# First feed-forward product: its weights in four blocks, with another order on SyncE, GpSimd and ScalarE

## The reference

```python
h = (rmsnorm(x, P['g_pre_ffn'][l]) * (1.0 + scale2) + shift2).astype(x.dtype)
up = h @ P['w_up'][l]                                  # 1024 -> 5632
up, ffn_conv_new = causal_dwconv(up, ffn_conv_prev, P['ffn_conv_w'][l])   # 3 taps
a, b = jnp.split(up.astype(f32), 2, axis=-1)
y = (jax.nn.gelu(a) * b).astype(x.dtype) @ P['w_down'][l]
```

## Time and profile before

| | |
|---|---|
| three runs | 1896.59, 1900.85, 1907.34 us; median 1900.85 |
| profiled execution | 1898.44 us, its span 1896.7 us |
| busy in the span | TensorE 1630.2, VectorE 946.4, GpSimd 737.6, ScalarE 591.9 us |
| granted TensorE clock, mean | 0.922 |
| largest GpSimd group | `lo`, L2433, 84 of 128x512 from the sums, mean 1536 ns |

### The profile page before, as it was taken

The page is one execution under the profiler, slowest core; times in us unless marked ns, Lnnn a source line. Parts: engine busy times, 40 slices in busy tenths (PEclk is TensorE's granted clock), DMA queues, the critical chain, the costliest instruction groups (busy, mean ns, idle before and its releaser), DMA issues. The chain is left out here.

```text
span 1896.7 us, 27581 instructions
## 1 busy us (share of the span) xinstructions
PE 1630.2 (86%) x10719; PEld 1426.4 (75%) x10719; DVE 946.4 (50%) x1601; ACT 591.9 (31%) x1003; POOL 737.6 (39%) x925
## 2 busy tenths in 40 slices
PE   5799988999788777998796589999999995999997
PEld 2568886899566545897674589988899995778886
DVE  1551027630556444454344856666666665555553
ACT  2431132221344341232243243333333332332322
POOL 1531022221100027853023777777777773211111
PEclk7899988999799977897898789999999998999999
DMA  8425422230311067321331111111111111855562
GB/s 322 139 90 202 141 88 82 70 94 33 103 59 45 18 216 183 81 97 34 139 109 58 54 57 69 69 69 68 69 69 69 69 69 55 271 201 196 201 221 108
DMA packets 123043, 208.09 MB, mean 110 GB/s; under 512 B 37492, under 2 KB 85668, under 8 KB 119586
## 3 DMA queue, kind: packets, MB, share of 16 engines
q1 hardware_dynamic: 120450, 197.42, 31.8%
q10 hardware_dynamic: 2464, 8.91, 1.2%
HBM read 163.26 MB, written 42.91 MB: 109 GB/s over the span
## 5 line engine op out<-in xcount | busy, mean ns | idle before, releaser
L2645 DVE SCALAR_TENSOR_TENSOR fu_tmp<-fu_zp,fu_cw,fu_tmp 128x1024 f32<-128x1024 f32 x88 | 121.8, 1384 | 176.3 <-ACT fu_tmp L2579 174.7
L2400 PE MATMUL fu_ps<-fu_thi,fu_whi 128*128 128x272 f32 (+2 forms) x672 | 144.8, 298 | 38.0 <-DVE fu_zp L2662 38.0
L2872 PE MATMUL fd_ps<-fd_whi,fd_yhi 128*128 128x512 f32 x396 | 123.6, 394 | 25.5 <-DVE fd_wlo L2926 20.8
L2400 PE MATMUL fu_ps<-fu_tlo,fu_whi 128*128 128x272 f32 (+2 forms) x672 | 143.5, 296 | 0.0
L2400 PE MATMUL fu_ps<-fu_thi,fu_wlo 128*128 128x272 f32 (+2 forms) x672 | 143.1, 295 | 0.0
L2400 PEld LDWEIGHTS fu_ps<-fu_thi,fu_whi 128*128 128x128 f32 x672 | 110.9, 195 | 41.8 <-POOL fu_wlo L2433 41.2
L2433 POOL TENSOR_TENSOR fu_wlo<-fu_s,fu_whi 128x512 fp32r<-128x512 f32 x84 | 128.1, 1536 | 12.8 <-ACT fu_whi L2535 12.8
L2889 ACT ACTIVATE fd_whi<-fd_w 128x1024 fp32r<-128x1024 f32 x66 | 69.9, 1060 | 186.8 <-PE fd_ps L2872 148.0
L2433 POOL TENSOR_TENSOR fu_wlo<-fu_w,fu_whi 128x512 fp32r<-128x512 f32 x67 | 119.4, 1784 | 9.4 <-ACT fu_whi L2535 9.4
L2872 PE MATMUL fd_ps<-fd_wlo,fd_yhi 128*128 128x512 f32 x396 | 123.0, 392 | 0.0
L2400 PE MATMUL fu_ps<-h_hi,fu_whi 128*128 128x272 f32 (+1 forms) x504 | 105.7, 291 | 14.9 <-POOL fu_wlo L2433 14.9
(11 more groups left out here) (358 smaller groups left out, 3828.8 us busy)
## 6 DMA issues: line engine op xcount, KB each, us to landing
fd_w<-in_w_down SPq DMA_DIRECT2D x66, 512.0 KB, 4.8
wa<-in_w_ada SPq DMA_DIRECT2D x24, 1024.0 KB, 6.5
fu_w<-in_w_up SPq DMA_DIRECT2D x44, 512.0 KB
scr_y<-fu_tmp SPq DMA_DIRECT2D x22, 544.0 KB, 2.7
fd_y<-scr_y SPq DMA_DIRECT2D x44, 192.0 KB
fp_w<-in_w_fm SPq DMA_DIRECT2D x16, 512.0 KB, 3.7
scr_qkv<-fp_y SPq DMA_DIRECT2D x9, 512.0 KB, 2.9
dr_stg<-scr_qkv SPq DMA_DIRECT2D x8, 576.0 KB, 5.9
```

The lines of the kernel that those rows point to most:

```text
L2400: last = pe.matmul(lane_of(q, o)[:, n, 0:size], w[:, o, kk], part(low, kk, slice(c, c + size)), start=(kk == 0 and m == 0), stop=(kk == HK ...
L2645: one = dve.scalar_tensor_tensor(yp, a, w, yp, ALU.mult, ALU.add)
L2872: last = pe.matmul(ps[OUT_BANK[p][n]][:, c:c + 512], y[:, k, n * P:(n + 1) * P], w[:, k, c:c + 512], start=(f == 0 and m == 0), stop=(f == ...
```

## The change

The buffer of raw weights and four semaphores, one per block, are made before `output_projection`, and SP issues the four loads (256 KB each) of unit 0 at the end of its list there. In `ffn_up` every block is loaded by itself, with a wait for its own last reader. The sums and parts get the order A11, S3, S2, S1, A12, S4, A22 on GpSimd and ScalarE; TensorE keeps its order of products and waits for the place of its operand in the new one (`split_at`). `first_tap(j,0)` moves ahead of the high part of S4.

```diff
@@ output_projection, SP, after the last load of x
+            for m in range(2):
+                for k in range(2):
+                    c = slice(KD // 2 * k, KD // 2 * (k + 1))
+                    sp.dma_start(K.w_up_raw[:, m, c], K.w_up_d[m, :, c]).then_inc(K.w_up_in[2 * m + k], 16)
@@ ffn_up
+        ORDER = (A11, S3, S2, S1, A12, S4, A22)
+        raw11_in, raw12_in, raw21_in, raw22_in = K.w_up_in
+        def split_at(j, o):
+            return splits(j) + (ORDER0 if j == 0 else ORDER).index(o) + 1
...
-            def load(j):
-                after(sp, lo_set, splits(j))
-                for m in range(2):
-                    sp.dma_start(raw[:, m], K.w_up_d[2 * j + m]).then_inc(raw_in, 16)
+            def load(j, m, k):
+                sp.dma_start(raw[:, m, HK * k:HK * k + HK], K.w_up_d[2 * j + m, :, HK * k:HK * k + HK])\
+                    .then_inc(K.w_up_in[2 * m + k], 16)
+
+            def load_front(j):
+                if j == 1:
+                    sp.wait_ge(lo_set, split_at(0, A21))
+                else:
+                    sp.wait_ge(lo_set, split_at(j - 1, A11))
+                    sp.wait_ge(s_set, 4 * (j - 1) - 1)
+                load(j, 0, 0)
+                load(j, 1, 0)
+
+            def load_back(j):
+                sp.wait_ge(lo_set, split_at(j - 1, A12))
+                if j > 1:
+                    sp.wait_ge(s_set, 4 * (j - 1))
+                load(j, 0, 1)
+                sp.wait_ge(lo_set, split_at(j - 1, A22))
+                load(j, 1, 1)
 
             def store(j):
                 sp.wait_ge(y_set, j + 1)
                 sp.dma_start(K.scr_y[j], ybuf(j)).then_inc(K.y_kept[j % 2], 16)
 
-            load(0)
             sp.dma_start(prev[:], K.fprev_d).then_inc(small_in, 16)
             sp.dma_start(cw[:], K.fconv_d).then_inc(small_in, 16)
-            load(1)
-            for j in range(KF):
-                if 0 < j < KF - 1:
-                    load(j + 1)
-                if j:
-                    store(j - 1)
+            load_front(1)
+            load_back(1)
+            for j in range(1, KF):
+                if j + 1 < KF:
+                    load_front(j + 1)
+                store(j - 1)
+                if j + 1 < KF:
+                    load_back(j + 1)
...
             def front_sums(j):
-                pool.wait_ge(raw_in, 32 * (j + 1))
-                pool.wait_ge(lo_set, splits(j))
+
+                if j > 1:
+                    pool.wait_ge(lo_set, split_at(j - 1, S2))
+                    pool.wait_ge(s_set, 4 * (j - 1))
+                pool.wait_ge(raw11_in, 16 * (j + 1))
+                pool.wait_ge(raw21_in, 16 * (j + 1))
+                pool.tensor_tensor(sums[:, 1], a11, a21, ALU.subtract).then_inc(s_set, 1)
+                if j > 1:
+                    pool.wait_ge(lo_set, split_at(j - 1, S4))
+                pool.wait_ge(raw22_in, 16 * (j + 1))
                 pool.tensor_tensor(sums[:, 0], a21, a22, ALU.add).then_inc(s_set, 1)
-                pool.wait_ge(s_set, 4 * (j - 1) + 1)
+
+            def middle_sum(j):
+                pool.wait_ge(lo_set, split_at(j, S3))
+                pool.wait_ge(s_set, 4 * (j - 1) + 2)
                 pool.tensor_tensor(sums[:, 1], sums[:, 0], a11, ALU.subtract).then_inc(s_set, 1)
 
-            def back_sums(j):
-                pool.wait_ge(lo_set, splits(j) + S1 + 1)
-                pool.wait_ge(s_set, 4 * (j - 1) + 2)
+            def back_sum(j):
+                pool.wait_ge(lo_set, split_at(j, S1))
+                pool.wait_ge(s_set, 4 * (j - 1) + 3)
+                pool.wait_ge(raw12_in, 16 * (j + 1))
                 pool.tensor_tensor(sums[:, 0], a12, sums[:, 1], ALU.subtract).then_inc(s_set, 1)
-                pool.wait_ge(s_set, 4 * (j - 1) + 3)
-                pool.tensor_tensor(sums[:, 1], a11, a21, ALU.subtract).then_inc(s_set, 1)
...
             for j in range(1, KF):
                 more = j + 1 < KF
-                if more:
-                    front_sums(j + 1)
                 halo(j, 0)
                 if more:
                     lo(j + 1, A11)
+                    front_sums(j + 1)
+                    lo(j + 1, S3)
+                    middle_sum(j + 1)
                     lo(j + 1, S2)
                     lo(j + 1, S1)
-                    back_sums(j + 1)
+                    back_sum(j + 1)
                 halo(j, 1)
-                if more:
-                    lo(j + 1, S3)
                 copies(j, 1)
                 if more:
                     lo(j + 1, A12)
-                    lo(j + 1, S4)
                 copies(j, 0)
                 if more:
+                    lo(j + 1, S4)
                     lo(j + 1, A22)
...
-            high(0)
             hi(0, A11)
             hi(0, A12)
+            high(0)
             high(1)
             hi(0, A21)
             hi(0, A22)
...
                 first_tap(j - 1, 1)
                 gelu(j - 1)
                 if more:
-                    for o in (A11, S2, S1, S3, A12, S4):
+                    for o in (A11, S3, S2, S1, A12):
                         hi(j + 1, o)
                 first_tap(j, 0)
                 if more:
+                    hi(j + 1, S4)
                     hi(j + 1, A22)
```

More of the change, by code:

```diff
@@ L2270, in ffn_up @@
         SPLIT = {A11: EVEN, S2: EVEN, S1: EVEN, S3: BACK, A12: EVEN, S4: BACK, A22: EVEN}
-        raw = sb("fu_w", [P, 2, KD, P])
+        raw = K.w_up_raw
         w_hi = sb("fu_whi", [P, PROD, HK, P], F32R)
@@ L2283, in ffn_up @@
         ps = [own.enter_context(nc.psum_tensor(f"fu_ps{i}", [P, 2, 512], F32)) for i in range(4)]
-        (raw_in, small_in, hi_set, lo_set, s_set, f_set, td, th_set, l4_set, mm0, mm, tap_set, e0_set, p1_set, c11_set, u2_set, u3_set, u4_set, c22_set,
+        (small_in, hi_set, lo_set, s_set, f_set, td, th_set, l4_set, mm0, mm, tap_set, e0_set, p1_set, c11_set, u2_set, u3_set, u4_set, c22_set,
          c12_set, c21_set, chain_s, conv_a_set, conv_b_set, gelu_set, y_set, zero_set, halo_a, halo_b, copied_a, copied_b,
          st_out) = (sem("fu_" + n) for n in (
-             "raw_in small_in hi_set lo_set s_set f_set td th_set l4_set mm0 mm tap_set e0_set p1_set c11_set u2_set u3_set u4_set c22_set "
+             "small_in hi_set lo_set s_set f_set td th_set l4_set mm0 mm tap_set e0_set p1_set c11_set u2_set u3_set u4_set c22_set "
              "c12_set c21_set chain conv_a_set conv_b_set gelu_set y_set zero_set halo_a halo_b copied_a copied_b "
@@ L2390, in product @@
             def product(q, o, part):
-                pe.wait_ge(lo_set, splits(q + 1) + o + 1)
+                pe.wait_ge(lo_set, split_at(q + 1, o))
                 lane_free(q, o)
@@ L2430, in lo @@
             def lo(j, o):
-                n = splits(j) + (ORDER0.index(o) if j == 0 else o)
-                pool.wait_ge(hi_set, n + 1)
+                pool.wait_ge(hi_set, split_at(j, o))
                 pool.tensor_tensor(w_lo[:, o], block_of(j, o), w_hi[:, o], ALU.subtract).then_inc(lo_set, 1)
             def front_sums(j):
-                pool.wait_ge(raw_in, 32 * (j + 1))
-                pool.wait_ge(lo_set, splits(j))
+                if j > 1:
[7 more added lines that the diff above has]
+                pool.wait_ge(raw22_in, 16 * (j + 1))
                 pool.tensor_tensor(sums[:, 0], a21, a22, ALU.add).then_inc(s_set, 1)
-                pool.wait_ge(s_set, 4 * (j - 1) + 1)
+            def middle_sum(j):
+                pool.wait_ge(lo_set, split_at(j, S3))
+                pool.wait_ge(s_set, 4 * (j - 1) + 2)
                 pool.tensor_tensor(sums[:, 1], sums[:, 0], a11, ALU.subtract).then_inc(s_set, 1)
-            def back_sums(j):
-                pool.wait_ge(lo_set, splits(j) + S1 + 1)
-                pool.wait_ge(s_set, 4 * (j - 1) + 2)
+            def back_sum(j):
+                pool.wait_ge(lo_set, split_at(j, S1))
+                pool.wait_ge(s_set, 4 * (j - 1) + 3)
+                pool.wait_ge(raw12_in, 16 * (j + 1))
                 pool.tensor_tensor(sums[:, 0], a12, sums[:, 1], ALU.subtract).then_inc(s_set, 1)
-                pool.wait_ge(s_set, 4 * (j - 1) + 3)
-                pool.tensor_tensor(sums[:, 1], a11, a21, ALU.subtract).then_inc(s_set, 1)
             def whole(c):
@@ L2490, in _ @@
             lo(1, A11)
+            lo(1, S3)
+            middle_sum(1)
             lo(1, S2)
             lo(1, S1)
-            back_sums(1)
-            lo(1, S3)
+            back_sum(1)
             lo(1, A12)
@@ L2524, in hi @@
             def hi(j, o):
-                if o in (A11, A12, A22) or j == 0:
-                    act.wait_ge(raw_in, 32 * (j + 1))
+                if j == 0:
+                    act.wait_ge({A11: raw11_in, A12: raw12_in, A21: raw21_in, A22: raw22_in}[o], 16)
+                elif o in (A11, A12, A22):
+                    act.wait_ge({A11: raw11_in, A12: raw12_in, A22: raw22_in}[o], 16 * (j + 1))
                 else:
-                    act.wait_ge(s_set, 4 * (j - 1) + {S1: 1, S2: 2, S4: 3, S3: 4}[o])
```

(7 more changed lines are left out.)

## The result

Slower: 1974.11 us (median of 4 runs, 1968.91 to 1976.19) against 1899.04 before; ratio 1.038, 95% interval 1.034 to 1.042. The prediction was 1952 in 1912 to 1984. The profiled execution took 1976.19, its span is 1974.4: 77.7 more than before.

The account below looks back on a forecast made before the run. The prediction took GpSimd's work plus one bare load to bound the old kernel's round. Twenty rounds at 26.5 make 530 us (+53.5); with +2 and -2, 1898.4 becomes 1952, range 1912 to 1984.

Parts of the forecast that it names:

- The ring: Steady rounds: a22's load queues behind store(j-1), which waits for VectorE's product(j-1); this closes a loop of 26.5 us a round.
- rival D: Steady rounds: a22 arrives in time, GpSimd never waits, TensorE's 21.27 us sets the round; 1847 us, chance 0.03.
- fixed terms: Steps of one round besides landing and convolutions: 3.9, 1.58, 1.40, 0.79, 1.42, 1.45 and 1.28 us.
- rival B: Steady rounds: everything collides, product too, or blocks land at 5.7; rounds of 27.2 to 29, 1966 to 2002 us, chance 0.18.
- The landing: SP's store and two back loads after product, until a22 can be used: 4.85 us, bounds 3.5 to 5.7.
- The convolutions: VectorE's two convolutions per round, slowed by turns with GpSimd: 9.8 us together, 6.1 if free.
- values of before: The two convolutions' times in the old kernel's trace, 5.29 and 3.96, 9.25 us together; a round of 25.9.
- TensorE's clock: TensorE in steady rounds: some show a halved clock, at no cost unless more than 5.2 us is lost.
- Start and end: Before product(0): +2 us (bounds -4 to +4); after product(20), with TensorE further ahead: -2 us (bounds -4 to 0).
- The Trainium skill's estimate: Landing of the back blocks: last 256 KB about 3.4 us after product, a round of 25.1, the time 1924 us.

Follow-up runs that it names:

- the run with the wait alone: Changed kernel where SP still waits for product(j-1) ahead of the back blocks, but issues the store itself behind them: 1958.57 us, ratio 1.033.

## Why the prediction was right

- **The ring** was the step that decided, and it is shown: open it and the time falls to 1847, close it in the old kernel and that one slows by 9%. That 1847 is also rival D's figure is partly luck: D had rounds of 21.27 and put nothing outside them; measured were rounds of 20.97, and 9.5 us more outside them.
- **Its fixed terms** held to 0.1: 3.9 from the sum with a22 to the high part of S2 (1395.88 to 1399.78), 1.57 to the tap, 1.41 to the convolution, 0.80 and 1.42 around the second tap, 1.44 and 1.28 at the end (1389.10 gives 1390.38).
- **The band.** The measured round, 27.63, and time lie not in the band named the forecast (25.9 to 27.2, 1940 to 1966, chance 0.45) but in rival B's (27.2 to 29, 1966 to 2002, chance 0.18). B asked for all steps to collide, `product` too, or for blocks landing at 5.7. Neither came in full: `product` took 1.28 as before. The mechanism was right, and two of its terms were too small:
- **The landing**: 4.85 forecast, 5.37 (median) measured. In the turn shown a22, the third DMA in a row, took 0.79 to issue, twice what I counted. That this makes the difference is argued, not shown; a22 issued before a12 landed at 4.76.
- **The convolutions**: 9.8 forecast, 3.97 + 6.53 = 10.5 (medians). Laid out by turns I had 4.25 + 5.85 = 10.1, and I took less than my own layout. In the second, I left out S3's sum, the one just before GpSimd waits for a22: the trace shows four collisions, with the low parts of S4 (1408.34), A22 (1409.60) and A11 (1411.97) and with that sum (1413.22). My "values of before", 9.25, came from one round whose second convolution took 3.96; the median of the 20 rounds is 2.92, so that value should have been 8.2. Together with the landing this is 1.2 a round; the round was 27.63 where 26.5 was forecast, 23 us in all, nearly the whole of the difference between 1952 and the profiled execution's 1976.
- **TensorE's clock** cost nothing, as forecast. It fell around the waits of 3 to 4 us, and TensorE's busy time in the 20 rounds rose from 438.5 to 467.8 us, to 23.4 a round. That is still under 27.63, and VectorE, which is on the ring, waited for TensorE 0.3 us in all.
- **Start and end**: forecast +2 and -2, measured +0.9 (1111.55 against 1110.63) and +0.6 (from the last of these products to the end 310.2 against 309.6). TensorE began at 1046.33 in place of 1053.87 and restarted on unit 1 at 1094.30 in place of 1094.72: the gain was taken up there, as forecast. I had expected TensorE's lead to shorten the end; it did not.
- **The Trainium skill's estimate.** By the Trainium skill ("DMA: Bandwidth & Descriptors", section Anatomy of one DMA) a DMA that GpSimd issues takes about 2.0 us plus its bytes over 436 GB/s, by estimate 2.6 us for 256 KB; so I had 3.4 us after `product` and 1924. The trace agrees for the first of two front blocks, which SP issues with no store just ahead: 2.4 to 3.3 us from issue to landing, median 2.5. It does not agree for a12 behind the store, 3.5 to 5.0, median 4.0. The measured 5.37 decides.

## What to carry to other kernels

In a queue that is served in order, a load inherits the wait of every store in front of it. Before splitting a load to issue it earlier, write down what each entry ahead of it waits for, and follow that event back: if it depends on the data the load brings, the loop is closed and no round can be shorter than it. Here the split and the new order paid 52 us, and one store two lines too high turned that into a loss of 75. Idle time taken from one engine does not all come off the round: in the old order GpSimd's wait lost 2.0 a round and the round 0.66, since its instructions then met VectorE's.

## What the runs showed that I had not expected

Three DMAs issued back to back from SP did not take equal times to issue. With the store first, the third took about 0.8 us where the first two took 0.33 to 0.43, in 13 of the changed kernel's 20 rounds and in 18 of 20 of the old kernel with the store first. In six more rounds of the changed kernel the second took 1.2 to 1.9 instead. With the store behind both loads (the run with the wait alone) the third took 0.43 in every round, but the second took 0.9 to 1.5 in six. I did not test what makes the difference.
